# Two transformer blocks on one core: memory keys and values moved into the even mixer, decay and state parameters moved beside up stages, one root for two norms, inputs taken as they come

## The reference

```python
def mem_cross_attention(h, mem, norm_mem, w_q, w_kv, w_o):
    m = rms_norm(mem, norm_mem)
    q = (h @ w_q)...
    k, v = jnp.split(m @ w_kv, 2, axis=-1)      # no part of h
    ...softmax(q k^T * 256**-0.5) @ v...
    return o @ w_o

def even_mixer(h, cos, sin, ...):
    z = h @ w_in
    u, cq, ckv, kr = jnp.split(z, [512, 768, 896], axis=-1)
    y_pool = pool_mixer(u, pool_w, pool_scale)          # running means over 2, 4, 8, 16 tokens
    q = (rms_norm(cq, q_norm) @ w_q_up)...
    kv = (rms_norm(ckv, kv_norm) @ w_kv_up)...
    ...8 heads, causal softmax...
    return jnp.concatenate([y_pool, y_att], axis=-1) @ w_out

# odd mixer: xb = causal conv; gates r, i; log_a = -8 * r * softplus(-lam); scan; y = gelu(gate) * h
# end of block 1: rms_norm(x, final_norm); block 2 starts with rms_norm of that, times (1 + sc) plus sh
# S5: dt = exp(log_dt); decay = exp(a_re*dt); ab = decay * (cos, sin)(a_im*dt); coef = (ab - 1)/a; bb = coef * b
# FFN: (silu(h @ w_gate) * (h @ w_up)) @ w_down;  2816 features
```

## Time and profile before

| what | us |
|---|---|
| median of 3 runs (1838.22 to 1840.58) | 1839.5 |
| the profiled execution | 1842.75 |
| its span, first to last instruction | 1840.9 |
| PE busy in it | 1705.3 (93%) |
| DVE busy | 807.8 (44%) |
| ACT busy | 298.7 (16%) |
| POOL busy | 61.8 |
| mean granted clock of PE | 0.958 |

### The profile page before, as it was taken

The page is one execution under the profiler, slowest core; times in us unless marked ns, Lnnn a source line. Parts: engine busy times, 40 slices in busy tenths (PEclk is TensorE's granted clock), DMA queues, the critical chain, the costliest instruction groups (busy, mean ns, idle before and its releaser), DMA issues.

```text
span 1840.9 us, 21539 instructions
## 1 busy us (share of the span) xinstructions
PE 1705.3 (93%) x8586; PEld 1438.4 (78%) x8586; DVE 807.8 (44%) x1732; ACT 298.7 (16%) x660; POOL 61.8 (3%) x72
## 2 busy tenths in 40 slices
PE   7388999999998999999989899899999877999998
PEld 5267768888877885888878786588888766888887
DVE  6754234221255422522298567555543274343300
ACT  2031021000015112100001221522220011122200
POOL 0000000000000000000075000000000000000000
PEclk9589999999999999999999899999999967999999
DMA  6026736665634464666644233044444401444445
GB/s 215 34 75 220 275 134 221 229 226 199 215 137 164 168 243 157 211 244 223 214 138 137 69 118 123 24 165 156 149 149 149 130 20 60 147 149 149 152 145 172
DMA packets 82901, 290.19 MB, mean 158 GB/s; under 512 B 13297, under 2 KB 13297, under 8 KB 82033
## 3 DMA queue, kind: packets, MB, share of 16 engines
q1 hardware_dynamic: 82800, 288.81, 46.0%
HBM read 286.67 MB, written 1.05 MB: 156 GB/s over the span
## 4 chain that ended last, share of the span: by engine, by line
PE 84%; DVE 11%; issue 2%; DMA 1%; ACT 1%; SPq 1%; DVEq 0%; ACTq 0%
PE acc L375 70%; PE acc L438 4%; PE acc L420 3%; DMA ring<-stream 1%; PE score L565 1%; PE acc L541 1%; DVE rstd L1260 1%; PE turned L576 1%; PE score L521 1%; DVE H L1324 1%; SPq L342 0%; PE acc L589 0%; PE score L623 0%; DVE probs L1410 0%; PE score L736 0%
## 5 line engine op out<-in xcount | busy, mean ns | idle before, releaser
L375 PE MATMUL acc<-H,ring 128*128 128x256 f32 x3520 | 779.9, 384 | 32.0 <-DMA ring<-stream 13.6
L375 PEld LDWEIGHTS acc<-H,ring 128*128 128x128 f32 x3520 | 673.5, 192 | 136.6 <-DMA ring<-stream 14.8
L375 PE MATMUL acc<-FFN,ring 128*128 128x256 f32 x1408 | 310.3, 384 | 11.2 <-DVE X L1342 8.5
L375 PEld LDWEIGHTS acc<-FFN,ring 128*128 128x128 f32 x1408 | 270.7, 193 | 50.1 <-DVE X L1342 8.9
L375 PE MATMUL acc<-big,ring 128*128 128x256 f32 x952 | 208.2, 380 | 4.0 <-DVE big L1397 1.7
L375 PEld LDWEIGHTS acc<-big,ring 128*128 128x128 f32 x952 | 180.2, 190 | 31.4 <-issue 3.2
L1479 DVE SCALAR_TENSOR_TENSOR bT<-bT,cond 128x1024 f32<-128x1024 f32 x84 | 107.8, 1284 | 90.8 <-DMA bT<-ada_in 84.2
L1521 DVE TENSOR_TENSOR FFN<-pair,acc 128x256 f32<-128x256 f32 x42 | 17.7, 421 | 206.4 <-PE acc L375 206.4
L1559 DVE SCALAR_TENSOR_TENSOR pair<-acc,cols,pair 128x255 f32<-128x255 f32 x84 | 40.5, 482 | 121.5 <-ACT pair L1039 118.2
L1344 DVE SCALAR_TENSOR_TENSOR X<-acc,mod,X 128x256 f32<-128x256 f32 x24 | 11.6, 484 | 152.9 <-PE acc L375 152.7
L1039 ACT ACTIVATE pair<-acc,cols 128x256 f32<-128x256 f32 x84 | 47.0, 562 | 162.1 <-PE acc L375 162.1
(11 more groups left out here) (395 smaller groups left out, 1327.2 us busy)
## 6 DMA issues: line engine op xcount, KB each, us to landing
ring<-stream SPq DMA_DIRECT2D x440, 512.0 KB, 3.3
bT<-ada_in SPq DMA_DIRECT2D x96, 512.0 KB, 4.4
big<-ssm_in SPq DMA_DIRECT2D x2, 1024.0 KB, 5.6
cols<-cols_in SPq DMA_DIRECT2D x1, 1169.5 KB, 7.5
X<-x_in SPq DMA_DIRECT2D x1, 1024.0 KB, 4.9
MEM<-mem_in SPq DMA_DIRECT2D x1, 1024.0 KB, 12.4
FFN<-H SPq DMA_DIRECT2D x32, 32.0 KB, 1.9
y_out<-X SPq DMA_DIRECT2D x1, 1024.0 KB, 3.9
```

The costliest lines, as they stand in the source:

```text
L375: mm = nc.tensor.matmul(dst, w[:, k * cols_per:(k + 1) * cols_per], r, start=first and n == 0, stop=last and n == len(src) - 1)
```

## The change

The stage list takes `xk0` and `xv0` out of the cross attention and puts them between `ev_in` and `q_up`, and between `q_up` and `kv_up`. Their results go to `FFN` (`K0`, `V0`), the gained tiles, the pooled means, the angles and the diagonals to other buffers. The norm sums of the query part are taken inside `xk0` (after its tile 3), those of the key part inside `xv0` (after its third slot). DVE scales the memory before the angles; the pooled means move behind the 8 heads of `q_up`. The row blocks of `ada_w` are spread by a table: 4 instead of 18 with `xq0`, 36 instead of 22 with `up0` (one after each of its first 28 slots, DVE taking 2 in each of 14 steps).

`lru_parameters` moves to step 17 of `up0`. `state_parameters` is cut in pieces at steps 2, 8, 11 and 14 to 19 of `up1`; ACT's two sines for it move to step 4. POOL's instructions on 128 x 2048 become four each on 128 x 512.

Between the blocks DVE takes one root of the product of both variances; the first norm's own root follows later. `down` waits before each third of its first tile, `glu` before each multiply of its first tile, and `first_tile` gives `ev_out`, `xo0`, `xo1`, `do` a first tile whose multiplies wait one by one.

```diff
 STAGES = [
-    ("ev_in", 8, 8), ("q_up", 2, 8), ("kv_up", 1, 10), ("pool", 1, 4), ("att0", 0, 4), ("ev_out", 8, 8),
-    ("xq0", 8, 8), ("xk0", 8, 8), ("xv0", 8, 4), ("att1", 0, 8), ("xo0", 8, 8),
+    ("ev_in", 8, 8), ("xk0", 8, 8), ("q_up", 2, 8), ("xv0", 8, 4), ("kv_up", 1, 10), ("pool", 1, 4), ("att0", 0, 4),
+    ("ev_out", 8, 8), ("xq0", 8, 8), ("att1", 0, 8), ("xo0", 8, 8),
...
-ADA_WITH = [("ev_out", 4), ("xq0", 18), ("xo0", 4), ("up0", 22), ("down0", 6), ("od_xb", 4),
-            ("xq1", 12), ("xo1", 4), ("up1", 22)]
+ADA_SLOTS = [
+    ("ev_out", range(0, 8, 2)), ("xq0", range(1, 8, 2)), ("xo0", range(0, 8, 2)),
+    ("up0", list(range(28)) + list(range(28, 44, 2))), ("down0", range(0, 24, 4)), ("od_xb", range(0, 8, 2)),
+    ("xq1", range(0, 24, 2)), ("xo1", range(0, 8, 2)), ("up1", range(0, 44, 2)),
+]
...
+            def first_tile(name, src, arrived, base):
+                w = slot_in(name, 0)
+                bank_free(TILE0[name])
+                for k in range(KD):
+                    pe.wait_ge(arrived, base + k + 1)
+                    mm = nc.tensor.matmul(acc[TILE0[name] % 4][:, 0:S], w[:, k * P:(k + 1) * P], at(src, k),
+                                          start=k == 0, stop=k == KD - 1)
+                mm.then_inc(slot_used, 1)
...
             def down(name):
-                pe.wait_ge(ffn_mid, 2 + 22 * (int(name[-1]) + 1))
...
+                        if k == 0:
+                            pe.wait_ge(ffn_mid, 2 + 22 * int(name[-1]) + hi)
...
+            linear("xk0", M, fresh, between=query_sums)      # query_sums: norm(2, False) after tile 3
+            pe.wait_ge(norm_out, outs[0])
             for s in range(2):
                 w = slot_in("q_up", s)
...
+            values("xv0", M, key_sums)                       # key_sums: norm(1, False) after slot 2
+            pe.wait_ge(norm_out, outs[0])
             w = slot_in("kv_up", 0)
...
-            def values(name):
+            def values(name, dst, between=None):             # ACT
                 begin(name)
                 for half in range(2):
                     act.wait_ge(slot_used, RING + SLOT0[name] + 4 * half + 4)
+                    if half and between:
+                        between()
...
+            squares(6, 1)
+            values("xv0", V0, variance_root)
...
             def swiglu(name, layer):                         # DVE
...
-                    ada(1)
+                    ada(2 if layer == 0 and k < 14 else 1)
+                    if layer == 0 and k == 17:
+                        lru_parameters()
+                    if layer == 1 and k in (2, 8, 11):
+                        (state_angles if k == 2 else state_decays if k == 8 else input_factors)()
+                    if layer == 1 and 14 <= k < 20:
+                        input_product(k - 14)
...
                 if layer:
-                    state_parameters()
                     shift_columns(0, 0, gained_in_late)
...
-            inverse_rms(rstd[:])
             norms[0] += 1
-            own(v.tensor_tensor(r2, rstd[:], rstd[:], ALU.mult))
-            dve.wait_ge(norm_sums, norms[0])
-            own(v.tensor_tensor(r2, stat[:, S:2 * S], r2, ALU.mult))
-            v.tensor_scalar(variance[:], r2, 1.0 / D, EPS, ALU.mult, ALU.add).then_inc(norm_vars, 1)
+            dve.wait_ge(norm_sums, norms[0] + 1)
+            own(v.tensor_scalar(first_var, stat[:, 0:S], 1.0 / D, EPS, ALU.mult, ALU.add))
+            own(v.tensor_scalar(both, stat[:, S:2 * S], 1.0 / D, None, ALU.mult))
+            v.scalar_tensor_tensor(variance[:], first_var, EPS, both, ALU.mult, ALU.add).then_inc(norm_vars, 1)
             dve.wait_ge(norm_rstd, norms[0])
-            inverse_root(r2)
-            own(v.tensor_tensor(both, r2, rstd[:], ALU.mult))
+            inverse_root(both)
```

More of the change, by code:

```diff
@@ L672, in _ @@
                            lambda h, c: V[:, c * D + h * VH:c * D + (h + 1) * VH])
-            outs[0] += 4
-            pe.wait_ge(acc_free, 4 + TILE0["ev_out"])
-            linear("ev_out", Y)
+            first_tile("ev_out", Y, acc_free, TILE0["att0"])
+            linear("ev_out", Y, first=1)
             mem_attention(0)
@@ L693, in _ @@
             outs[0] += 4
[L694 to L700, removed]
+            first_tile("od_out", Y, lru_out, 0)
             linear("od_out", Y, first=1)
@@ L878, in _ @@
                 bank_free(TILE0["glu"] + k)
-                b = acc[(TILE0["glu"] + k) % 4]
-                product(b[:, 0:S], w, [at(MEM, i) for i in range(KD)]).then_inc(slot_used, 1)
+                for n, i in enumerate(S5_ORDER):
+                    if k == 0:
+                        pe.wait_ge(s5_gelu, n + 1)
+                    mm = nc.tensor.matmul(acc[(TILE0["glu"] + k) % 4][:, 0:S], w[:, i * P:(i + 1) * P], at(MEM, i),
+                                          start=n == 0, stop=n == KD - 1)
+                mm.then_inc(slot_used, 1)
             up("up3", lead([("up3", 0), ("up3", 1)], gained_in_ffn, S + 1))
@@ L1026, in swiglu @@
                         .then_inc(silu_done, 1)
+                    if i == 1 and k == 4:
+                        for e in range(2):
+                            sine_of()
+                            nc.scalar.activation(small[:, (10 + e) * 32:(11 + e) * 32],
+                                                 small[:, (8 + e) * 32:(9 + e) * 32], ACT.Sin).then_inc(sines, 1)
             def conv_ffn(name, layer):
@@ L1112, in _ @@
             swiglu("up1", 1)
-            for e in range(2):
-                sine_of()
-                nc.scalar.activation(small[:, (10 + e) * 32:(11 + e) * 32], small[:, (8 + e) * 32:(9 + e) * 32],
-                                     ACT.Sin).then_inc(sines, 1)
             double_norm()
@@ L1234, in _ @@
             own(ins)
-            own(g.tensor_scalar(whole, r, ROUND, ROUND, ALU.add, ALU.subtract))
-            own(g.tensor_tensor(r, r, whole, ALU.subtract))
+            quarters = [slice(512 * q, 512 * q + 512) for q in range(4)]
+            for q in quarters:
+                own(g.tensor_scalar(whole[:, q], r[:, q], ROUND, ROUND, ALU.add, ALU.subtract))
+            for q in quarters:
+                own(g.tensor_tensor(r[:, q], r[:, q], whole[:, q], ALU.subtract))
             for st in range(STATE_TILES):
@@ L1239, in _ @@
             own(ins)
-            own(g.tensor_tensor(r, r, whole, ALU.add))
-            own(g.tensor_scalar(r, r, 0.5, -0.5, ALU.min, ALU.max))
+            for q in quarters:
+                own(g.tensor_tensor(r[:, q], r[:, q], whole[:, q], ALU.add))
+            for q in quarters:
+                own(g.tensor_scalar(r[:, q], r[:, q], 0.5, -0.5, ALU.min, ALU.max))
             pool.sem_inc(s5_angle, 1)
@@ L1753, in _ @@
             dve.sem_inc(kr_done, 1)
-            norm(Y, 2, lambda k: col("q_norm", k), H, first=4, features=256)
             begin("q_up")
@@ L1887, in _ @@
                 dve.sem_inc(idx_roped, 1)
+            dve.wait_ge(norm_rstd, norms[0])
+            inverse_root(rstd[:])
             for k in range(KD):
```

324 lines of the change are left out of this document (182 added, 142 removed).

## The result

| | median, us | lowest to highest | profiled run | its span | its mean clock |
|---|---|---|---|---|---|
| before | 1839.5 | 1838.2 to 1840.6 | 1842.75 | 1840.9 | 0.958 |
| after | 1781.95 | 1780.7 to 1783.8 | 1783.83 | 1782.1 | 0.975 |

The ratio is 0.9688, with a 95% interval of 0.9672 to 0.9705. The change is 57.5 us faster, 58.9 between the two profiled runs. Forecast were 60.4 and a time of 1779.1; the time measured is 2.9 us above it.

A forecast was written before the change was run, and what follows sets the result against it. PE's own work was taken as the bound (84% of the span), so only its stops and the low clock behind them could be won. Terms -28.7, 0, -6.3, -10.3, -5.8, -9.3 sum to -60.4: median 1839.5 to 1779.1 us, range 1768 to 1799.

The forecast's parts named there:

- 1 keys and values: Mixer: `xk0` and `xv0` fill PE's waits there, 55.4 us leave the cross attention, `kv_up` starts at 117.5; -28.7 us.
- 2 row blocks: `xq0` loses its ring-slot wait (4.67 + 1.7 us), but it comes back in `up0` at the same price; 0.
- 3 `lru_parameters`: Moved from `od_xb` to `up0` step 17, hidden there; `od_xb`'s 4.38 us wait and slow multiplies go; -6.3 us.
- 4 state parameters: Pieces in `up1` no longer hold PE in `down1` (-10.8 us); 0.5 us put for step 8; -10.3 us.
- 5 one root: Between the blocks, 3.1 of PE's 4.28 us wait and 2.7 us of low clock go; -5.8 us.
- 6 inputs as they come: First tiles of `down3`, `glu`, `ev_out`, `do`, `xo0`, `xo1` start without waiting for all inputs; -9.3 us, `down3` -5.8 of it.
- rival A: In `up0`, row blocks set the pace: loop 8.5 us instead of 6.94, +22 over 14 steps, 1801; chance 0.12.
- rival C: In `up0`, each step's blocks hold the ring as the first does: +83 us, 1862, slower than before; chance 0.03.
- one of the prediction's signs of being wrong: In `up1`, a PE idle would show the forecast wrong; no size given.
- Rival D: DVE overruns in `up1` steps 2 and 8 and `up0` step 17, about 4 us each: 1791; chance 0.12.
- Rival B: PE at half work from 71 to 83 us gets 1.2 GHz, held through `xv0`: up to +27, 1806; chance 0.05.

The follow-up runs named there:

- root_early: Changed kernel with ACT taking the key norm's root before its wait for the last slots of `xv0`; median 1776.4 us, ratio 0.9654.
- blocks_late: Changed kernel with row blocks later in SP's queue, in `up0` (third behind slot 5, not 2) and `od_xb`; median 1768.2 us, ratio 0.9610.
- table_whole: Changed kernel with POOL's table instructions 2048 columns wide again instead of four times 512; median 1781.6 us, ratio 0.9687.
- two_roots: Changed kernel with a root for each of the two norms behind `down1` again; median 1788.7 us, ratio 0.9712.
- early_only: Changed kernel with `lru_parameters`, state parameters, two roots and single first-tile waits put back, POOL's quarters and the rest kept; median 1808.6 us, ratio 0.9820.
- state_back: Changed kernel with the state parameters made in one go between `up1` and `down1` again, POOL's quarters kept; median 1790.2 us, ratio 0.9719.
- best1: Changed kernel with the key norm's root sooner, row blocks later in SP's queue and `state_decays` cut in two; median 1761.1 us, ratio 0.9577.
- after_again: Changed kernel run once more with nothing edited; median 1781.5 us, ratio 0.9676.

## Why the prediction was right, term by term

| term | forecast | measured | from |
|---|---|---|---|
| 1 keys and values | -28.7 | -31.5 | a, less `xq0`'s wait (4.67 + 1.66) and a first tile (0.53) |
| 2 row blocks | 0 | +1.8 | b +7.3, first tile of `xo0` 0.85, less the 6.3 of `xq0` |
| 3 `lru_parameters` | -6.3 | -5.3 | c |
| 4 state parameters | -10.3 | -9.9 | e -10.7; in d +0.85 |
| 5 one root | -5.8 | -5.5 | f |
| 6 inputs as they come | -9.3 | -9.7 | j -6.15, `glu` 0.8, first tiles 0.53, 0.53, 0.85, 0.85 |
| nowhere in the sum | 0 | +1.3 | g -2.35, h +1.3 and a first tile 0.53, i +1.8 |
| sum | -60.4 | -58.8 | |

**Term 1** was the one mis-sized most. `kv_up` came at 116.13, not 117.5, mostly because the kernel's start with its first sums was 1.0 us shorter (the two sums took 1.06 and 1.00 in before, 0.64 and 0.59 in after). Behind it, `att0` took 23.0 us up to `ev_out`, and 24.0 in before without the wait of 0.53 there. Neither goes with the change: over the other kernels here the start differs by 1.3 us and `att0` lies between 22.5 and 24.0, so some 2 of the 2.8 us are not the term's. The rest is the wait before `att1`, which fell from 1.18 to 0.47, as ACT's wide copies no longer stand there; `att2`, where they do, still has 1.18. I had not counted that. The parts of the working came out: DVE's pace of 1.80 a head set `xv0`'s start, `xv0` lost 1.9 us at the low clock (29.9 for 27.48 and the sums), and the chain behind the key norm's root was open for 4.5. root_early shows that this chain was the place of one instruction.

**Term 2.** The wait came back where it was forecast, and only once: rival A (the blocks set the pace) and rival C (lock step, 1862) are out, and blocks_late settles why. The size was off: 5.19 us and 2.5 behind it, instead of 4.67 and 1.7; the first multiplies ran at half clock, with DMA at 349 GB/s beside them. The windows of after (us, busy PE, PEld, DVE, ACT, POOL, clock, DMA share, GB/s), behind both stops:

```profile
267.00:271.00 4.00, 3.99 (x9) 3.19 (x10) 1.28 (x1) 0.00 (x0) 0.00 (x0) 0.50 0.98 349
271.00:275.00 4.00, 4.00 (x16) 3.37 (x15) 1.11 (x2) 0.00 (x0) 0.00 (x0) 0.76 0.98 360
...
514.00:518.00 4.00, 4.00 (x10) 3.19 (x11) 0.65 (x1) 0.00 (x0) 0.00 (x0) 0.50 1.01 407
```

In the earlier trace rows the same span of 4 us behind the stop had 0.58. The 1.7 us that I took for "the low clock behind a stop" was a single reading.

**Term 3.** The second wait went, as forecast. The wait that stays cost 0.9 more behind it (48 records in 13.05 are 2.6 over; before, 32 in 8.66 were 1.7 over). The mis-sized part is the clock again.

**Term 4.** `down1` fell to what its multiplies take. The stop in `up1`'s step 8 that I had put at 0.5 us was 0.87. Its cause was half seen: I gave the cut into quarters the credit of capping the hold, but it also ended POOL's work later, and there it did harm (table_whole). By that stop one of the prediction's signs of being wrong, a PE idle in `up1`, did come. Rival D (4 us each) got a fifth of its price at one of its three places. And the 8.50 us were made in good part by POOL, not by the state parameters alone, which I had from one row and did not follow up; the term came out right because both went together.

**Terms 5 and 6** came out within 0.4 us, the first confirmed by two_roots. Of the second, early_only confirms `down3`'s wait (2.7) but has 1.8 us of low clock behind it, not 3.2: the size was met in part because before happened to have the longer one. For the first tiles alone no run was made.

**Rival B** (the low clock through `xv0`) is out: behind the first 24 records `xv0` runs at full clock.

So the forecast's mechanisms were right. The 1.6 us between -60.4 and -58.8 are a sum of errors with both signs: -2.8, +1.8, +1.0, +0.4, +0.3, -0.4 and +1.3. That they nearly cancel is luck; about 2 us of it is what the same instructions differ by from trace to trace. One sum of the prediction was off: its upper bounds add up to -39, which is 1800.5 and not 1799.

## What to carry to other kernels

A wait for a transfer is often a wait of the queue that issues it: see behind what instruction the issue stood, and put the item that depends on a late engine behind those that don't. An instruction that needs little and is needed soon (a root) belongs ahead of its engine's next wait for a long stage. Cutting one engine's instruction into pieces helps its neighbour only where they meet; it costs some time by itself (5.3 us for 4.5 here), and the later end can meet the neighbour elsewhere.

## What the runs showed of the hardware

In these traces a short stop of PE cost its length, and in some of them a further 1 to 2.4 us at the low clock. In after and in table_whole the last index tile waits the same 1.26 us for the same reason. After, windows behind it:

```profile
981.00:985.00 4.00, 4.00 (x39) 4.00 (x38) 0.07 (x1) 0.88 (x3) 0.00 (x0) 1.00 0.41 131
985.00:989.00 4.00, 3.35 (x25) 2.43 (x24) 0.00 (x0) 3.26 (x6) 0.00 (x0) 1.00 0.00 0
```

table_whole, windows behind it:

```profile
979.00:983.00 4.00, 4.00 (x30) 4.00 (x30) 0.00 (x0) 0.56 (x2) 0.00 (x0) 0.76 0.41 131
983.00:987.00 4.00, 4.00 (x19) 3.40 (x20) 0.00 (x0) 2.13 (x5) 0.00 (x0) 0.50 0.00 0
```

The same work took 13.9 us at 2.4 GHz, and 16.3 in part at 1.2. This is column g; columns h (218.2 to 220.8) and i (83.1 to 85.3) have the same behind stops of 1.5 to 2.4 us. In state_back and in best1 the stop before `down2` is 1.96 us; from there to its sums it took 79.1 us in the one and 77.5 in the other. Within one kernel, i was 85.2 and then 83.1 (after_again). Nothing in the edits goes with the choice, but the moment at which the stop comes does differ from run to run. What decides it was not shown; g and h were the same in both executions of after, so for them a kernel's own timing is not ruled out. So a difference of 2 us between two single traces, behind a stop, is not yet the change's; what the stop's own length changed by can be read at once.

POOL and DVE: one instruction of POOL with two inputs of 128 x 2048 took 4.51 us, one of 128 x 512 took 1.27 unheld and 2.13 beside DVE's multiply-add; DVE's two-input instruction of 128 x 32 took 1.03 us instead of 0.19 beside a quarter, its 128 x 512 one 1.64 and 4.88 instead of 0.69 beside 512 and 2048 columns.
